# A ring of weight buffers moved 128 bytes down against the tensors it is multiplied with

## The reference, cut to what matters

```python
def swiglu(x, w_gate, w_up, w_down):
    return (jax.nn.silu(x @ w_gate) * (x @ w_up)) @ w_down
...
        f = swiglu(rms_norm_2(h, ffn1_norm_pre[l]), ffn1_w_gate[l], ffn1_w_up[l], ffn1_w_down[l])
        h = h + 0.5 * rms_norm_2(f, ffn1_norm_post[l])
```

## The kernel before

| tensor | address | past a multiple of 2048 | of 512 |
|---|---|---|---|
| `x_res` | 10368 | 128 | 128 |
| `raw0` and `w_lo0` (five more, each 4096 further) | 26752 | 128 | 128 |
| `w_hi0` (five more, each 4096 further) | 51328 | 128 | 128 |
| `sq0`, `sq1`, `ht0` ... `rn` | 75904 and up | 128 | 128 |
| `x_hi`, `x_lo`, `h_hi`, `h_lo`, `rec_hi`, `m_hi`, `at_hi` | 92288 and up | 128 | 128 |
| `lru_xc`, `lru_wx`, `lru_wa` (float32, layer 3) | 192640, 209024, 217216 | 128 | 128 |
| `nsa_p` (layer 2) | 187680 and up | 1312 | 288 |
| `swa_p` (layer 1) | 195104 and up | 544 | 32 |
| `dil_pt` (layer 3) | 225600 | 320 | 320 |

## Time and profile before

### The profile page before, as it was taken

How to read it: one execution, slowest core, us unless ns; L and a number is a source line. 1 busy time by engine, 2 the same in 40 slices (tenths; PEclk the granted TensorE clock), 3 DMA queues, 4 the chain that set the end, 5 groups by cost and what they waited for, 6 DMA issues and landing times.

```text
span 2775.8 us, 38492 instructions
## 1 busy us (share of the span) xinstructions
PE 2722.0 (98%) x16358; PEld 2254.0 (81%) x16358; DVE 1447.8 (52%) x2372; ACT 1064.4 (38%) x1620; POOL 15.6 (1%) x30
## 2 busy tenths in 40 slices
PE   9988999999999999999999999999999999999998
PEld 7787788888887778888888888886888788888887
DVE  6834576552625666756336443374634544654433
ACT  5534454332324664433224222245433522432221
POOL 0000000000000000000000000001000000000000
PEclk9999999999999999999999999999999999999999
DMA  4200122223431001322222223236222223232232
GB/s 160 90 4 3 38 91 97 94 98 99 144 117 46 1 1 61 122 93 98 99 91 97 94 99 99 95 120 129 80 86 82 71 96 99 80 110 93 97 99 68
DMA packets 68685, 238.84 MB, mean 86 GB/s; under 512 B 7800, under 2 KB 10360, under 8 KB 68004
## 3 DMA queue, kind: packets, MB, share of 16 engines
q1 hardware_dynamic: 62256, 220.80, 23.7%
q10 hardware_dynamic: 6260, 15.59, 2.5%
HBM read 228.23 MB, written 6.03 MB: 84 GB/s over the span
## 4 chain that ended last, share of the span: by engine, by line
PE 92%; DVE 4%; ACT 3%; issue 1%; DMA 0%; ACTq 0%; DVEq 0%
PE psum L155 23%; PE psum L157 23%; PE psum L156 23%; PE psum L1322 3%; PE psum L1289 2%; PE psum L1309 2%; PE psum L843 2%; PE psum L201 2%; PE psum L202 1%; PE psum L209 1%; PE psum L1817 1%; PE psum L1953 1%; PE psum L177 1%; PE psum L178 1%; PE psum L176 1%
## 5 line engine op out<-in xcount | busy, mean ns | idle before, releaser
L155 PE MATMUL psum<-x_hi,w_hi 128*128 128x512 f32 x2128 | 844.7, 397 | 0.6 <-DVE w_lo L130 0.6
L157 PE MATMUL psum<-x_hi,w_lo 128*128 128x512 f32 x2128 | 829.1, 390 | 0.0
L156 PE MATMUL psum<-x_lo,w_hi 128*128 128x512 f32 x2128 | 828.2, 389 | 0.0
L130 DVE TENSOR_TENSOR w_lo<-raw,w_hi 128x1024 fp32r<-128x1024 f32 x409 | 500.0, 1225 | 391.2 <-ACT w_hi L123 391.2
L123 ACT ACTIVATE w_hi<-raw 128x1024 fp32r<-128x1024 f32 x409 | 427.9, 1050 | 303.8 <-DMA raw<-w_down 83.1
L155 PEld LDWEIGHTS psum<-x_hi,w_hi 128*128 128x128 f32 x2128 | 399.6, 188 | 90.7 <-issue 5.6
L156 PEld LDWEIGHTS psum<-x_lo,w_hi 128*128 128x128 f32 x2128 | 399.8, 188 | 86.3 <-issue 5.0
L157 PEld LDWEIGHTS psum<-x_hi,w_lo 128*128 128x128 f32 x2128 | 399.4, 188 | 83.9
L155 PE MATMUL psum<-h_hi,w_hi 128*128 128x512 f32 x616 | 239.6, 389 | 0.0
L156 PE MATMUL psum<-h_lo,w_hi 128*128 128x512 f32 x616 | 239.6, 389 | 0.0
L157 PE MATMUL psum<-h_hi,w_lo 128*128 128x512 f32 x616 | 239.6, 389 | 0.0
(11 more groups left out here) (410 smaller groups left out, 3304.8 us busy)
## 6 DMA issues: line engine op xcount, KB each, us to landing
raw<-w_up SPq DMA_DIRECT2D x88, 512.0 KB, 3.3
raw<-w_down SPq DMA_DIRECT2D x44, 512.0 KB, 3.3
raw<-w_f1up SPq DMA_DIRECT2D x44, 512.0 KB, 3.3
raw<-w_f2up SPq DMA_DIRECT2D x44, 512.0 KB, 3.3
raw<-w_qkv SPq DMA_DIRECT2D x36, 512.0 KB, 3.4
raw<-w_blend SPq DMA_DIRECT2D x28, 512.0 KB, 3.2
raw<-w_f1down SPq DMA_DIRECT2D x22, 512.0 KB, 3.3
raw<-w_f2down SPq DMA_DIRECT2D x22, 512.0 KB, 3.2
```

The lines of the kernel that those rows point to most:

```text
L130: dve.tensor_tensor(self.w_lo[u % SLOTS][:], self.raw[u % SLOTS][:], self.w_hi[u % SLOTS][:].bitcast(F32), ALU.subtract).then_inc(self.lo_ ...
L155: pe.matmul(bank[:], hi, x_hi[:, kk], start=kk == 0, stop=False)
L156: pe.matmul(bank[:], hi, x_lo[:, kk], start=False, stop=False)
L157: mm = pe.matmul(bank[:], lo, x_hi[:, kk], start=False, stop=kk == kt - 1)
```

## The change

A constant `WEIGHTS_BEFORE` of 32 elements (128 bytes) is taken off the filler in front of `x_res`, and a new tensor of as many elements, which nothing reads or writes, is put behind the last `w_hi`.

```diff
-PAGE, FIRST = 512, 1056
+PAGE, FIRST, WEIGHTS_BEFORE = 512, 1056, 32
...
-        sb("to_a_page", [P, PAGE - (FIRST + dram["in_vec"].shape[1] + dram["in_const"].shape[1] + 2 * P + 30) % PAGE])
+        sb("to_a_page", [P, PAGE - (FIRST + dram["in_vec"].shape[1] + dram["in_const"].shape[1] + 2 * P + 30) % PAGE - WEIGHTS_BEFORE])
         k.x = sb("x_res", [P, KD, T])
         with ExitStack() as s:
             k.w_lo = [sb(f"w_lo{j}", [P, UB * P], F32R, s) for j in range(SLOTS)]
         k.raw = [sb(f"raw{j}", [P, UB * P]) for j in range(SLOTS)]
         k.w_hi = [sb(f"w_hi{j}", [P, UB * P], F32R) for j in range(SLOTS)]
+        sb("back_to_a_page", [P, WEIGHTS_BEFORE])
```

## The result

The changed kernel takes 2821.89 us, median of 4 runs (2820.77 to 2824.64), against 2775.49 us for the kernel before on the same chip: ratio 1.0169, 95% interval 1.0156 to 1.0182. It is 46 us slower. The forecast was 2774 us, no change, and the range ended at 2790 us.

A forecast was written before the change was run, and what follows sets the result against it. PE was taken to bound the kernel, by matmul count times step. Ring loads 0, ring traffic of ACT, DVE and DMAs 0, x_res 0 summed to no change: 2774 us by the median of runs, range 2738 to 2790 us.

The forecast's parts named there:

- What bounds the kernel: PE, busy 98% of the span: matmul count times step; one nanosecond on each of 9,816 ring matmuls is 9.8 us.
- The addresses: With rounding, the ring moves from 128 past a multiple of 512 to the multiple; moving row stays 128 past 2048.
- the term of the weight loads: PE's weight loads from the ring: 0 us taken, bounds -131 and +52 us.
- the 13.3 ns: Fixed part of each ring matmul with its weight load, beyond 512 columns at 0.417 ns; 131 us in all.
- the argument from line 1817: Float32 operands there, placed like ring and partner, show 2 ns beyond two cycles a column, so placing does not cause 13.3 ns.
- The upper bound: On ring steps: all as long as the dilated attention's slowest steady ones, 232 ns, 5.3 ns too long; +52 us.
- The slower rival: Ring load and moving row collide once 128 bytes apart; 2826 us at 5.3 ns, 2789 at 1.5; 0.15 with lost alignment.
- a lost alignment: Without rounding the ring would leave a multiple of 2048, a loss as large as the faster rival's gain; within the 0.15.
- The faster rival: Ring weight blocks stop straddling 512-byte pieces, so the fixed part shrinks; all 2643 us, a quarter 2741 us; chance 0.27.
- The covers: ACT, DVE and DMAs on the ring lie under PE, some 27 us a unit deep; cost 0.
- the 0 for `x_res`: ACT and DVE on x_res at the norm boundaries: cost 0, bounds -1 and +1 us.
- The signs given for the rival: Slower rival in the profile after: some of a unit's 24 steps longer than others, repeating with the block's place.

The follow-up runs named there:

- `e1_all_down`: Against the kernel before: x_res, the ring and every later tensor 128 bytes lower, distance between ring and activations kept; 2775.82 us, ratio 1.0001.
- `lru_apart`: Against the kernel before: a 128-byte filler between the moving lru_xc and stationary lru_wx, lru_wa of line 1817; 2773.96 us, ratio 0.9995.
- `e4_x_res_only`: Against the kernel before: only x_res 128 bytes lower, with a filler between it and the ring, which stays; 2775.39 us, ratio 1.0000.

## Why the prediction was wrong

**What bounds the kernel: right.** A count of matmuls times a step, and only what reaches the step matters. At 9.8 us per nanosecond the measured 5.8 ns would be 57 us; the span grew by 43.2. The starts in the two traces say where the difference lies. The ring has 9,336 matmuls of 512 columns, and some 9,120 of their steps hold no wait; these took 2070 us before and 2120 us after, 50 us more, 227.0 ns against 232.4 in the mean, since the kernel before has some slower steps too (below). The longer gaps in the ring's stream took 3 us less, the 256-column steps some 0.5 us less, and everything else 4 us less. Of the last part some may be the clock: the trace of before was granted 0.50 of it, the 1.2 GHz level, for some 27 us and the trace after for some 19 us.

**The addresses: right, and so was not believing the text of the change.** The ring does come to lie on a multiple of 2048. That it gained an alignment was of no use: `e1_all_down` has the same placing of the ring and gains nothing by it.

**The failed step: "I take 0, since the two rows that vary the offset and nothing else show 1 ns or less".** It put the term of the weight loads at nothing, and it measured 5.8 ns on each 512-column step. The rows were those of lines 1309 and 1953, and what separates fast from slow here is the distance between the two operands modulo 256 bytes. Line 1309 varied nothing of the kind: 288 and 32 past a multiple of 512 are both 32 past a multiple of 256. Line 1953 varied little: its `dil_pt` and `sq` are 64 bytes apart modulo 256, and with the moving `dil_vt`, which begins at 211072, `sq` has a distance near 0 and `dil_pt` one near 64, the one at which the ring too loses least, 0.4%. Both rows are float32, in which `lru_apart` shows no cost at 128 bytes, and have 128 or 129 columns, while the ring's own 256-column steps show no loss either. The text named the type as the hole in the argument, but priced it as small. None of the eight distances brings the mean 512-column step below 226.7 ns, so the 13.3 ns do not come from the placing, as the argument from line 1817 had said.

**The upper bound was met, as far as is shown by luck.** "Every step becomes as long as the slowest steady ones that the trace has", 232 ns, 2826 us; measured 232.5 ns and 2822 us. But the steps of the earlier trace rows are not steady. In the trace of before the ring's stream sets in at 98 places behind matmuls of other lines, and behind nearly every one of them the steps run through one fixed series, from its start or from a later member on: 233, 236, 224, 231, 236, 228, 233, 231 ns, give or take one. Then they stay at 226 or 227 ns. The first nine have a mean of 229.8 ns, all from the tenth on 226.7. The dilated attention, where such places are many, has its slow steps from this alone. In the changed kernel the stream never settles so: 232.1 ns in the first nine, 232.4 from the twentieth on. Whether the two are one effect is not shown.

**The slower rival was the right one, and weighed too low.** It named what the experiments show, equal low address bits lost, and had 0.15, together with a lost alignment, against 0.27 for the faster one. What misled in weighing it is the sentence that "within one unit the loads already start at four different places within 2048 bytes against the same moving row, and all steps are equal". It is true, and it only excludes a dependence on multiples of 512 bytes; the shift of the change is 128. Evidence from places that differ by 512 was used against an effect that repeats every 256, where it cannot speak. The other half, line 1953, fell with the stand-in.

**The faster rival** is excluded by `e1_all_down`: with the ring on a multiple of 512 and the distance kept, a triple is 680 ns, as before.

**The covers: right.** ACT, DVE and the DMAs on the ring (1050 ns, 1225 ns, 3.3 us to landing) did not change, and `e4_x_res_only` confirms the 0 for `x_res`.

**The signs given for the rival** were half right: a window with fewer matmuls, unequal steps. In the changed kernel they do not repeat with the place of the block but every seven steps; at distances of 64 and 96 they do follow the three matmuls of a block.

**What stays open.** That loads and rows disturb each other by their distance modulo 256 bytes is shown, from both sides. How they do is not. That a shifted load lengthens the next step too, that prices do not add, that a series of seven steps runs across units, and that with equal offsets the stream falls into equal steps after at most nine while at 128 it does not, speak for a relation in time between the two reads that moves on from step to step; this is argued, not shown. Why 64 bytes cost little and why 256-column and float32 steps do not suffer was not tried.

## What to carry to other kernels

In a stream of float32r matmuls with a weight load each, give the stationary and the moving operands of 512-column matmuls the same offset modulo 256 bytes: that distance, and not the alignment of either, was worth 0.4 to 2.5% here, and a filler of 32 bytes anywhere between them can lose it. Work out addresses with the allocator's rounding, and when a tensor is inserted or resized, check that the ring and all its partners still agree; a count of steps per window shows a loss at once, while the mean load (188 ns), the waits and the other engines look as before. When a row stands in for one that the trace lacks, it must share the type, the width and the period of the thing in question; a row that varies something by 256 or 512 says nothing about a shift of 128 when the effect repeats every 256.

## What the runs showed of the hardware that was not expected

The time of a TensorE step depends on how its two operands lie to each other in SBUF: with a distance of 32 to 224 bytes modulo 256 a 512-column float32r step goes from 226.7 to between 228 and 234 ns (200 us divided by 876 to 856 matmuls), at a granted clock of 1.00 and with no other engine changed. The Trainium skill, page "SBUF — State Buffer", section "Who interferes with whom", gives TensorE two read ports, one for the moving operand and an independent one for the weight load, and says "PE and ACT never wait on anyone." That sentence is about other engines, and the runs here do not contradict it: no other engine was seen to lengthen a step. With "independent" they do not agree: the same instructions in the same order lose up to 2.5% by the placing of those two operands alone, and the measurement decides.

The loss belongs to 512-column float32r steps: at 128 bytes they lose 5.8 ns, float32 steps of 512 columns show no cost, and 256-column float32r steps can get shorter where the 512-column ones get longer (a mean of 117.0 and 233 ns at 192 bytes, 119.7 and 226.7 ns at 0).

A float32r stream of the kernel before needs up to nine steps behind matmuls of other lines, with a mean of 229.8 ns, before it settles at 226.7 ns.
